# One transformer layer on one core: four copies and sums of the mixer stage in another place, tiles scaled by ScalarE

## The reference

```python
h = rmsnorm(x, norm1_gain) * (1.0 + scale1) + shift1          # c_act @ w_ada + b_ada gives the six columns
proj = h @ w_in                                               # q (512) | k, v (2 x 128) | p (512)
attn_out = sliding_window_attention(q, k, v, q_gain, k_gain, attn_sinks, rel_bias_table)
pool_out = multiscale_pool(p, w_pool, pool_scale)             # windows 2, 4, 8, 16: mean minus self
merged = concat(rmsnorm(attn_out, attn_out_gain), rmsnorm(pool_out, pool_out_gain))
x = x + gate1 * (merged @ w_out)
h2 = rmsnorm(x, norm2_gain) * (1.0 + scale2) + shift2
ffn = (silu(h2 @ w_gate) * (h2 @ w_up)) @ w_down
x = x + gate2 * ffn
```

## Time and profile before

| | us |
|---|---|
| median of 3 runs | 961.57 (960.68 to 962.08) |
| profiled execution, its own time | 960.69 |
| its span | 958.9 |
| TensorE busy | 925.3 (96%) |
| VectorE busy | 787.7 (82%) |
| ScalarE busy | 520.0 (54%) |
| GpSimd busy | 281.6 (29%) |

### The profile page before, as it was taken

The page is one execution under the profiler, slowest core; times in us unless marked ns, Lnnn a source line. Parts: engine busy times, 40 slices in busy tenths (PEclk is TensorE's granted clock), DMA queues, the critical chain, the costliest instruction groups (busy, mean ns, idle before and its releaser), DMA issues.

```text
span 958.9 us, 14047 instructions
## 1 busy us (share of the span) xinstructions
PE 925.3 (96%) x4345; PEld 768.0 (80%) x4345; DVE 787.7 (82%) x1239; ACT 520.0 (54%) x1003; POOL 281.6 (29%) x243
## 2 busy tenths in 40 slices
PE   6988999979999999999999999999999999999998
PEld 5776888868887777888888888888888888888886
DVE  5969999988689969787787977879688787977797
ACT  4545665666344645555464654646465464655553
POOL 0025364441100100703306061240704216060334
PEclk9999999999999999999999999999999999999999
DMA  9975644356345495657456546644656556556624
GB/s 355 389 228 207 247 167 141 110 175 222 132 131 176 150 329 201 210 194 255 157 191 227 213 176 219 214 180 175 225 195 236 183 192 236 177 177 217 219 88 176
DMA packets 96136, 193.97 MB, mean 202 GB/s; under 512 B 6513, under 2 KB 57441, under 8 KB 96097
## 3 DMA queue, kind: packets, MB, share of 16 engines
q1 hardware_dynamic: 90816, 182.05, 54.4%
q10 hardware_dynamic: 5280, 11.45, 3.4%
HBM read 176.30 MB, written 17.17 MB: 202 GB/s over the span
## 4 chain that ended last, share of the span: by engine, by line
PE 75%; DVE 15%; DMA 4%; issue 3%; ACT 2%; SPq 0%; POOL 0%; ACTq 0%; DVEq 0%; POOLq 0%
PE ps L2158 24%; PE ps L2160 24%; PE ps L2159 24%; DVE stage L1391 2%; DMA raw_u<-in_w_up 1%; DVE wo_raw L1488 1%; DMA bs<-bs_scratch 1%; DVE nmax L1630 1%; DVE s_sb L1629 1%; DVE xs L1522 1%; PE ps L2401 1%; DMA wi_raw<-in_w_in 1%; DVE acc L1404 1%; DMA x_st<-in_x 1%; ACT ht_hi L745 1%
## 5 line engine op out<-in xcount | busy, mean ns | idle before, releaser
L1335 POOL TENSOR_TENSOR x<-x,p1s 128x512 f32<-128x512 f32 x80 | 117.2, 1485 | 421.6 <-ACT p1s L1032 421.1
L2158 PE MATMUL ps<-bs,ring 128*128 128x512 f32 x344 | 134.7, 392 | 2.7 <-ACT ps L960 1.4
L2160 PE MATMUL ps<-bs,ring 128*128 128x512 f32 x344 | 134.1, 390 | 0.0
L2159 PE MATMUL ps<-bs,ring 128*128 128x512 f32 x344 | 134.0, 390 | 0.0
L1772 DVE TENSOR_TENSOR ring<-s,ring 128x512 fp32r<-128x512 f32 x88 | 68.8, 801 | 50.2 <-ACT ring L953 50.2
L2158 PE MATMUL ps<-h_hi,ring 128*128 128x512 f32 x272 | 106.2, 391 | 0.6 <-DVE h_lo L1765 0.6
L2159 PE MATMUL ps<-h_lo,ring 128*128 128x512 f32 x272 | 106.0, 390 | 0.0
L2160 PE MATMUL ps<-h_hi,ring 128*128 128x512 f32 x272 | 105.9, 389 | 0.0
L953 ACT ACTIVATE ring<-s 128x512 fp32r<-128x512 f32 x88 | 53.8, 623 | 66.5 <-PE ps L2160 66.5
L2158 PEld LDWEIGHTS ps<-bs,ring 128*128 128x128 f32 x344 | 64.6, 188 | 18.7 <-issue 2.3
L2158 PE MATMUL ps<-wi_hi,ht_hi 128*128 128x512 f32 (+1 forms) x192 | 70.1, 365 | 6.6 <-DVE wi_lo L1576 5.2
(11 more groups left out here) (298 smaller groups left out, 2341.6 us busy)
## 6 DMA issues: line engine op xcount, KB each, us to landing
bs<-bs_scratch SPq DMA_DIRECT2D x166, 512.0 KB, 6.1
raw_g<-in_w_gate SPq DMA_DIRECT2D x11, 1024.0 KB, 5.4
raw_u<-in_w_up SPq DMA_DIRECT2D x11, 1024.0 KB, 7.9
raw_d<-in_w_down SPq DMA_DIRECT2D x20, 512.0 KB, 4.3
ada_in_raw<-in_w_adat SPq DMA_DIRECT2D x16, 512.0 KB, 9.2
stage<-in_w_adat SPq DMA_DIRECT2D x16, 512.0 KB, 5.5
wi_raw<-in_w_in SPq DMA_DIRECT2D x8, 640.0 KB, 10.3
stage<-in_w_ada SPq DMA_DIRECT2D x8, 512.0 KB, 6.8
```

Of the source, the lines that this page charges most:

```text
L1335: pool.tensor_tensor(x1_half(t, 1), x1_half(t, 1), p1s[j][:, :], ALU.add).then_inc(pool_evac, 1)
L2158: pe.matmul(dst, s_hi, m_hi, start=start, stop=False, skip_group_check=onto)
L2159: pe.matmul(dst, s_hi, m_lo, start=False, stop=False, skip_group_check=onto)
L2160: return pe.matmul(dst, s_lo, m_hi, start=False, stop=stop, skip_group_check=onto)
```

## The change

- `square_x(2)` leaves the end of turn 0 and stands in turn 1 behind the copies of q, k and p of tile 0.
- `FOLDS` puts two GATE1 folds from turn 1 into turn 2, and two others from turn 2 into turns 3 and 4. `sum_gate1` and its `take` stand in turn 3 instead of 2, the SCALE2 `take` in 5 instead of 4.
- `scale_x` of tiles 4 to 7 leaves VectorE. ScalarE does it, `scale_rows`, at the end of the turn before, as eight activations of 128 x 128 with a column of a1 as factor, in place. `h_high` goes in front of `square_qk`.
- For z from 1 to 5 the first half of the probabilities is transposed ahead of the pool product instead of behind it, and ScalarE copies in the same order.
- In turn 7 the low parts of W_out rows 0 and 1 and the scaling of row 5 go from before q's normalisation to behind the copy of p.

```diff
@@ -248,11 +248,13 @@
         pieces = [(mm, k) for mm in BG for k in range(KT)]
 
 
-        FOLDS = (3, 5, 4, 4, 4, 4, 0, 0)
+        FOLDS = (3, 3, 4, 5, 5, 4, 0, 0)
         SCALED = ((), (), (), (), (), (0, 1), (2, 3, 4), (5,), (6, 7))
-        TAKEN = {2: GATE1, 4: SCALE2, 6: SHIFT2}
+        TAKEN = {3: GATE1, 5: SCALE2, 6: SHIFT2}
         assert sum(FOLDS) == len(BG) * KT
 
+
+        PROBS_FIRST = range(1, NT - 2)
 
         HALF0 = (0, 1, 3, 5)
         HALF1 = (2, 4, 6, 7)
@@ -739,6 +741,12 @@
                 act.wait_ge(hlo_done, KT + t - 2)
                 act.dma_start(xs_of(t), xt[t]).then_inc(xt_in[t % 2], 16)
 
+            def scale_rows(t):
+                xt_landed(act, t)
+                for k in range(KT):
+                    last = act.activation(xs_of(t)[:, k, :], xs_of(t)[:, k, :], ACT.Copy, scale=a1[:, k:k + 1])
+                last.then_inc(xs_done, 1)
+
             def h_high(t):
                 act.wait_ge(xs_done, t - 1)
                 act.wait_ge(p_chain, t - 1)
@@ -808,6 +816,14 @@
                     act.wait_ge(pv_done, 2 * (t - 1) + ch + 1)
                 act.activation(pt_sb[:, ch], bank4(5 + ch), ACT.Copy).then_inc(pt_evac, 1)
 
+            def evac_y(t):
+
+                act.wait_ge(y_done, t + 1)
+                if t >= 1:
+                    act.wait_ge(mixed_out, 16 * t)
+                    act.wait_ge(sqm_done, t)
+                act.activation(mT[:, NPR:KT, :], bank4(7), ACT.Copy).then_inc(y_evac, 1)
+
             def evac_o(t, ch):
 
                 act.wait_ge(pv_done, 2 * t + ch + 1)
@@ -856,12 +872,12 @@
                     keep_shift(0)
                     keep_shift(1)
                     keep_shift(2)
-                if 0 <= z:
-                    act.wait_ge(y_done, z + 1)
-                    if z >= 1:
-                        act.wait_ge(mixed_out, 16 * z)
-                        act.wait_ge(sqm_done, z)
-                    act.activation(mT[:, NPR:KT, :], bank4(7), ACT.Copy).then_inc(y_evac, 1)
+                if z in PROBS_FIRST:
+                    evac_pt(z, 0)
+                    evac_y(z)
+                    evac_pt(z, 1)
+                elif 0 <= z:
+                    evac_y(z)
                     evac_pt(z, 0)
                     evac_pt(z, 1)
                 if it == NT + 1:
@@ -890,6 +906,8 @@
                     if a >= 2:
                         act.wait_ge(mixp_done, a - 1)
                     act.activation(pext[:, a % 2, :, HALO:], bank4(7), ACT.Copy).then_inc(pT_evac, 1)
+                    if a == 0:
+                        square_x(2)
                 if 0 <= z and it != NT:
                     evac_o(z, 0)
                 if 1 <= a < NT - 1:
@@ -912,11 +930,11 @@
                 if it == NT - 1:
                     wo_high(2)
                 if it < NT - 1:
+                    if prepared(it):
+                        h_high(prepared(it))
                     square_qk(it)
                 if it == 0:
                     h_high(3)
-                if it < NT - 1 and prepared(it):
-                    h_high(prepared(it))
                 if 1 <= z and it < NT - 1:
                     evac_ssm(z - 1)
                 if 0 <= a < NT and it < NT:
@@ -937,10 +955,12 @@
                 if it == NT:
                     wo_high(4)
                     wo_high(5)
-                if it + 2 < NT:
+                if 1 <= it and it + 2 < NT:
                     square_x(it + 2)
                 if 1 <= it and it + 3 < NT:
                     load_xt(it + 3)
+                if prepared(it + 1):
+                    scale_rows(prepared(it + 1))
 
 
             def a_high(p, o, m, par, first=False):
@@ -1614,8 +1634,6 @@
                     h_low(2)
                     scale_x(3)
                     evac_q(0)
-                if prepared(it):
-                    scale_x(prepared(it))
                 if it in (0, 2, 3, 4, 5, 6):
                     evac_kv(it)
                 if 0 <= a < NT:
@@ -1671,10 +1689,6 @@
                 if 0 <= a < NT:
                     probs(a, 0)
                     probs(a, 1)
-                if it == NT - 1:
-                    wo_low(0)
-                    scale_wo(it)
-                    wo_low(1)
                 if it == NT:
                     mixed_sum(0, 0)
                     wo_low(4)
@@ -1700,6 +1714,10 @@
                     fold(1)
                 if 1 <= it < NT:
                     evac_p(it)
+                if it == NT - 1:
+                    wo_low(0)
+                    scale_wo(it)
+                    wo_low(1)
                 if it in TAKEN:
                     take(TAKEN[it], (0, 1))
                     if TAKEN[it] == SCALE2:
@@ -2316,7 +2334,11 @@
                     pe.wait_ge(hlo_done, KT + it)
                     pe.wait_ge(q_evac, it)
                     project(it, q_bank(it), slice(0, QW), q_chain)
-                if 0 <= z:
+                if z in PROBS_FIRST:
+                    transpose_probs(z, 0)
+                    pool_linear(z)
+                    transpose_probs(z, 1)
+                elif 0 <= z:
                     pool_linear(z)
                     transpose_probs(z, 0)
                     transpose_probs(z, 1)
@@ -2343,7 +2365,7 @@
                     if z == 0:
                         pe.wait_ge(q_evac, 2)
                         pe.wait_ge(p_evac, 2)
-                    if it == 3:
+                    if it == 4:
                         pe.wait_ge(mod_done, 1)
                     attend(z, 0)
                 if 0 <= a < NT:
@@ -2387,7 +2409,7 @@
                 if 3 <= it < NT:
                     pe.wait_ge(p_evac, it)
                     project(it, p_bank(it), slice(QW + KVW, IN), p_chain)
-                if it == 2:
+                if it == 3:
 
                     pe.wait_ge(o_evac, 2 * z + 2)
                     sum_gate1((0, 1))
```

## The result

The changed kernel took **977.31 us** (median of 6 runs, 973.71 to 980.59); the kernel before took 962.38 in the same session. The ratio is 1.0155, 95% interval 1.013 to 1.0179: slower by 1.6%. The forecast was 952.3 us, and the range ended at 956.6.

What follows compares the result with a forecast made beforehand. TensorE and VectorE were taken as full in the mixer stage's steady part, leaving TensorE's gaps; leads of 2.07, 5.8, 4.85, 4.2, 7.7 and 8.9 grew to 9.3 us, giving 952.3 us from the median 961.57; range 949.8 to 956.6.

Steps and rivals of the forecast that it cites:

- the sum: Mixer stage: the edits' leads carried to its last attend, counted as a gain of 9.3 us for the kernel.
- (e): Mixer stage tiles: small in-place ScalarE activations cost more than 0.30 us each, up to 974 us; chance 0.03.
- Square later: Before the first scores: TensorE's 3.07 us idle goes, VectorE's s_sb sets a lead of 2.07 us.
- GATE1 later: Tile 1: two folds moved start s_sb 3.7 us earlier, lead 5.8; the sum returns a tile later, costing 1.8.
- Scaling by ScalarE: Tiles 4 to 7: eight activations take 2.5 us in a 3.09 us hole; costs 1.2 at tile 2, lead 4.85.
- Rival (a): ScalarE sets the pace in each remaining tile, gain only 4.9 us, 956.7 us; chance 0.16.
- Probabilities first: Later mixer tiles: a 0.54 us hole before the q transposes goes in each; lead 7.7 by s_sb of tile 6.
- the ledger: The prediction's running account of leads through the mixer stage, from 2.07 us at the first scores to 9.3.
- W_out behind p: Last tile: q transposes lead by 11.2 us, VectorE's s_sb of tile 7 by 8.9, last attend by 9.3.
- The clock: TensorE at 72 to 76 and 210 to 215 us: full speed returns, about 3 us if TensorE alone counted; counted nothing.
- rival c: Mixer stage: the clock's return is worth 2 of its 3 us through unseen VectorE slack, 950.3 us; chance 0.08.

Runs made afterwards that it cites:

- e3: The whole changed kernel with a directive padding ScalarE's feed-forward loop to start at slot 0 of a block of 256: 953.03 us, ratio 0.9913 to the kernel before.
- e4: The kernel before with the same directive, ScalarE's feed-forward loop at slot 0 of a block of 256: 960.94 us, ratio 1.0002.
- b_hybrid: The changed kernel without directive, tile 4 scaled by VectorE in turn 3, the other three on ScalarE: 953.42 us, ratio 0.9924 to the kernel before.

## Why the prediction was wrong, step by step

**The step that failed** is the one ahead of the sum: "The lead at the last instruction of the stage is the gain, since what follows (from 232 us on) is released by this stage's products." What follows is also released by its instructions being there. I priced the 32 scaling activations by their time beside other work, 8 x 0.30 + 0.1 a tile, and never as 32 places in ScalarE's program ahead of a loop; every rival, the slower one (e) too, was about time in the mixer stage. The measured cost of that is 745.69 - 725.74 = 19.95 us between two profiles, and 977.31 - 953.03 = 24.3 between the medians of two sessions, whose kernels before differ by 1.1; the profile after was of one of the shorter executions (975.01). The hint was in the profile of before: a loop body of 260 ScalarE instructions, and only one packet on q14 in the 300 us from 500 to 800. What the forecast says of the mixer stage, with the stalls away, is to be read in e3: 953.03 us against the 952.3 of the forecast, a gain of 8.3 beside its session's 961.3 against one of 9.3. The rows below are of its timeline.

The leads below are counted from the profile that the prediction read. This was one execution, and its stage was a long one: in the profile of e4, with the same mixer code, the stage takes 164.51 us instead of 166.83, and TensorE's list has no wait on ht_lo and none on g1bc, which the sum had counted as some 1.3 us of gain. Counted from the stage's start in e4, e3's leads are 3.2 at the q transposes of tile 3, 4.5 at tile 6 and 5.3 at the last attend (7.1 from the span's start). So agreement with single terms below, to a microsecond, is in part luck; the 8.3 of the medians is the firmer number.

**Square later: right.** The first scores start at 67.20 with no idle before them; the 3.07 us of the earlier trace rows are gone. Counted from the stage's start it is a lead of 3.2. VectorE's s_sb now follows the folds directly, as the step said (VectorE sets it):

```profile
67.75 2.68 DVE L1425 SCALAR_TENSOR_TENSOR acc<-stage,cact,acc 128x1024 f32<-128x1024 f32 x2
70.35 0.68 DVE L1648 TENSOR_TENSOR s_sb<-ps,bias 128x512 f32<-128x512 f32 x1
```

That is 2.62 earlier than at 72.97, 2.15 from the stage's start, against 2.07. The size is in part luck. The 2.07 us that VectorE idled held some of the slow clock of that one execution; in the profile of e4 the same scores took 2.53 us instead of 3.61, and VectorE idled 1.19:

```profile
72.22 2.53 PE L2376 MATMUL ps<-kT,qbd 128*128 128x128 f32 x16 [3.10 <-ACT kT L836]
73.39 0.69 DVE L1630 TENSOR_TENSOR s_sb<-ps,bias 128x512 f32<-128x512 f32 x1 [1.19 <-PE ps L2376]
```

**GATE1 later: right.** s_sb of tile 1 was forecast "near 87":

```profile
87.14 0.69 DVE L1648 TENSOR_TENSOR s_sb<-ps,bias 128x512 f32<-128x512 f32 x1 [0.34 <-PE ps L2398]
```

The GATE1 sum is at 111.45, one tile later, with no wait, 1.88 us long (forecast: 1.8 of cost). VectorE waits 0.34 here, so the last folds of the earlier trace rows were not the only limit any more: TensorE had its own new wait, 2.10 us for mix_p at 78.14, near the place ("around 77 us") where the text expected one.

**Scaling by ScalarE: right in size and cost.** Eight took 2.45 us (forecast 2.5), and the q transposes of tile 2 came at 97.97 (forecast 97.45), waiting for ScalarE:

```profile
94.76 2.45 ACT L747 ACTIVATE xs<-xs,a 128x128 f32<-128x128 f32 x8 [0.90 <-ACT x_st L735]
97.23 0.60 ACT L817 ACTIVATE pt_sb<-ps 128x512 f32<-128x512 f32 x1
```

```profile
97.97 0.63 PE L2351 MATMUL ps<-ident,qn 128*128 128x128 f32 x4 [1.54 <-ACT pt_sb L817]
```

Rival (a), ScalarE at the limit in every tile, did not happen: this is the only pt_sb wait left. The prediction charged 1.2 us for it; b_hybrid takes the wait away and gains nothing; VectorE's product is back there (1.65 us, at 105.12), and waits on VectorE have grown instead.

**Probabilities first: right.** The wait of the earlier trace rows, six times 0.4, is down to that one, and TensorE is full where it was at 19.61, while VectorE has fallen from 19.52:

```profile
120.00:140.00 20.00, 20.00 (x122) 17.69 (x121) 17.65 (x41) 14.66 (x44) 9.36 (x11) 1.00 0.59 211
```

The prediction put each fold moved into tiles 3 and 4 at about 2 us, as much as the removed scaling. That did not come: the five folds of tile 3, from 119.53 on, took 1.22 or 1.23 us each, and in tile 4 only the last took longer, 1.86 us. VectorE was relieved there.

Leads at the q transposes, from the stage's start: 3.9 at tile 2, 4.0 at tile 3, 4.5, 4.9 and 6.1 at tiles 4 to 6; the ledger had 4.85, 4.2 and then half a microsecond more per tile to 6.3.

**W_out behind p: right in kind, its tail short by about 1.6.** The q transposes of tile 7 lead by 10.0 (forecast 11.2), with 0.35 us of idling instead of 3.82. VectorE's s_sb of tile 7 was to lead by 8.9; it starts at 209.05, 7.32 earlier than at 216.37, 6.9 from the stage's start. VectorE has not a gap there, and more work in front than was counted: two low parts ran as one group of 3.34 us,

```profile
204.66 1.22 DVE L1520 TENSOR_TENSOR h_lo<-m_raw,h_hi 128x1024 fp32r<-128x1024 f32 x1
205.79 3.34 DVE L1514 TENSOR_TENSOR wo_lo<-wo_raw,wo_hi 128x1024 fp32r<-128x1024 f32 x2
209.05 0.68 DVE L1648 TENSOR_TENSOR s_sb<-ps,bias 128x512 f32<-128x512 f32 x1
```

where two further on took 2.35. TensorE waited twice, as said, for VectorE (1.92 us on sq_s, 0.97 on h_lo). The last attend starts at 224.86, a lead of 8.1 against 9.3, 7.6 from the stage's start.

**The clock.** I counted nothing for it. In the stretches of the earlier trace rows, 0.72 and 0.66 of full speed, the run has full clock:

```profile
67.00:71.00 4.00, 4.00 (x34) 3.91 (x34) 3.90 (x4) 1.76 (x3) 2.73 (x4) 1.00 0.46 139
...
205.00:210.00 5.00, 5.00 (x33) 4.48 (x33) 4.97 (x5) 2.01 (x4) 4.38 (x4) 1.00 1.05 360
```

The sixteen scores take 1.95 us instead of 3.61. As the rule cited from the Trainium skill, page "TensorE: Matmul & The Clock Gate", section "What's actually happening", had it, the clock came back with the idles gone. Nothing beyond the ledger shows at the end (rival c), as VectorE sets both places; but "nothing" was not quite what the sum held for the clock, since its first term, 2.07, had some of it inside. The clock matters where TensorE alone sets the time: in the feed-forward loop, behind each of the three stalls.

## What to carry to other kernels

An edit is also a change of address for everything behind it on its engine. If an engine runs a long loop (here 260 instructions), count the instructions that an edit adds or removes ahead of the loop and compare the instruction packets in the table of DMA queues; idle time "issue" at the period of the loop is the sign. Judge such an edit, for better or worse, with the loop at a fixed place, or one measures the luck of its address: here the same change was +1.6% or -0.9%.

## What the runs showed of the hardware

- A loop of 260 ScalarE instructions had no stall at its three branches back from slots 0, 96, 112, 120, 128, 192 and 248 of a block of 256, with at most one packet on q14 between 560 and 920 us. From slot 126 it had 7.2 us of stall at each (in the changed kernel, with the same stalls, 5.0 and 2.0 in two pieces), 21.6 us on ScalarE and 22 on the span, and five packets of some 8 KB a turn, four of them around the branch back. All but slot 0 are single runs.
- 32 drains that do nothing, ahead of such a loop, cost 23 us; 16 of them in the changed kernel took 24 us away (a single run).
- Entering the loop past padding at slot 128, 192 or 248 cost one stall of 5.7 to 5.9 us on entering, and about 3 us of the whole; at slots 126 and 120 ScalarE stood 4.4 and 3.1 us near the entry, and at 0, 96 and 112 none was seen.
- A 7.2 us stall of ScalarE, 54% busy in the kernel before, cost TensorE 4.5 us of idling and then 3 to 5 us at a granted clock of 0.50 to 0.52, which lost 1.4 to 2.6 us more: 6.6 a stall in the last part of the span.
